# A decoder trunk with 32 experts: down-projection weights issued from GpSimd's queue instead of SyncE's

## What is computed

```python
def moe_ffn(xn, w_router, b_router, w1, b1, w2, b2):       # 256 + 16 tokens, top 4 of 32 experts
    logits = (tok_x @ w_router + b_router).astype(jnp.float32)
    top_logit, top_e = lax.top_k(logits, TOP_K)
    top_w = jax.nn.softmax(top_logit, axis=-1)
    ...
    def expert_block(blk):
        tok_blk, w_blk, e = blk
        hb = x_pad[tok_blk] @ w1[e] + b1[e]                 # w1[e]: 1024 x 2048, 8 MiB
        ob = clamped_swiglu(hb) @ w2[e] + b2[e]             # w2[e]: 1024 x 1024, 4 MiB
        return ob * w_blk[:, None].astype(ob.dtype)
```

## Time and profile before

| | |
|---|---|
| median of 3 runs | 1399.79 us (1399.71 to 1402.7) |
| profiled execution | 1400.83 us, of it 1399.0 us span |
| PE busy | 1337.8 us (96%) |
| DVE / ACT / POOL busy | 484.5 / 320.9 / 74.5 us |
| moved by DMA | 461.80 MB, mean 330 GB/s |
| SyncE's queue (q1) | 458.64 MB; GpSimd's queue (q0) 2.49 MB |
| granted TensorE clock | 1.00 of full in nearly the whole span |

### The profile page before, as it was taken

How to read it: one execution, slowest core, us unless ns; L and a number is a source line. 1 busy time by engine, 2 the same in 40 slices (tenths; PEclk the granted TensorE clock), 3 DMA queues, 4 the chain that set the end, 5 groups by cost and what they waited for, 6 DMA issues and landing times.

```text
span 1399.0 us, 18726 instructions
## 1 busy us (share of the span) xinstructions
PE 1337.8 (96%) x7131; PEld 652.9 (47%) x7131; DVE 484.5 (35%) x1217; ACT 320.9 (23%) x630; POOL 74.5 (5%) x88
## 2 busy tenths in 40 slices
PE   8999999999999999999999999999999999999995
PEld 5867778889994333333323222223222223333331
DVE  6847779998743212111211111111111211121112
ACT  4445547765321111111111011011001011011101
POOL 1000002322303000000000000000000000000000
PEclk9999999999999999999999999999999999999999
DMA  6332131334778899999999999999999999999995
GB/s 244 129 128 114 61 121 61 122 121 181 277 299 328 353 418 418 418 416 416 418 419 418 419 417 416 418 418 418 419 417 416 417 416 417 418 419 419 417 416 229
DMA packets 77410, 461.80 MB, mean 330 GB/s; under 512 B 6848, under 2 KB 6848, under 8 KB 41136
## 3 DMA queue, kind: packets, MB, share of 16 engines
q1 hardware_dynamic: 76608, 458.64, 80.8%
q0 software_dynamic: 752, 2.49, 0.5%
HBM read 460.05 MB, written 1.05 MB: 330 GB/s over the span
## 4 chain that ended last, share of the span: by engine, by line
PE 60%; DMA 19%; SPq 16%; DVE 2%; issue 2%; ACT 1%; ACTq 0%; DVEq 0%
PE bank L1299 57%; DMA ring<-w_dram 19%; SPq L405 9%; SPq L372 6%; PE bank L1614 1%; PE bank L1620 1%; PE bank L1425 1%; DMA work<-x_dram 0%; PE bank L1407 0%; PE bank L1636 0%; DVE split L887 0%; PE bank L1482 0%; DVE work L924 0%; PE bank L1326 0%; ACT split L553 0%
## 5 line engine op out<-in xcount | busy, mean ns | idle before, releaser
L1299 PE MATMUL bank<-ring,work 128*64 128x512 f32 (+3 forms) x2264 | 548.5, 591 | 34.5 <-DMA ring<-w_dram 32.1
L1299 PE MATMUL bank<-work 128*64 128x512 f32 (+7 forms) x2168 | 445.7, 558 | 6.2 <-issue 1.9
L1299 PEld LDWEIGHTS bank<-ring,work 128*64 128x64 f32 (+1 forms) x2264 | 176.7, 142 | 355.9 <-issue 259.7
L1299 PEld LDWEIGHTS bank<-work 128*64 128x64 f32 (+4 forms) x2168 | 151.3, 144 | 261.7 <-issue 245.6
L1247 DVE COPY work<-bank 128x256 f32<-128x256 f32 x32 | 13.6, 424 | 496.4 <-PE bank L1636 496.4
L1299 PE MATMUL bank<-hn_hi,split 128*128 128x256 f32 (+1 forms) x896 | 173.3, 289 | 0.9 <-DVE split L887 0.5
L1299 PEld LDWEIGHTS bank<-hn_hi,split 128*128 128x128 f32 x896 | 142.3, 190 | 1.7 <-issue 0.9
L1299 PE MATMUL bank<-hn_lo,split 128*128 128x256 f32 (+1 forms) x448 | 127.5, 285 | 0.0
L1221 DVE TENSOR_SCALAR work<-bank 128x256 f32<-128x256 f32 x64 | 24.2, 419 | 273.9 <-PE bank L1299 273.9
L887 DVE TENSOR_TENSOR split<-ring,split 128x1024 fp32r<-128x1024 f32 x80 | 99.1, 1240 | 26.0 <-ACT split L553 25.7
L739 ACT ACTIVATE work<-bank 128x512 f32<-128x512 f32 x32 | 19.1, 597 | 331.5 <-PE bank L1299 331.5
(11 more groups left out here) (250 smaller groups left out, 948.2 us busy)
## 6 DMA issues: line engine op xcount, KB each, us to landing
ring<-w_dram SPq DMA_DIRECT2D x256, 1024.0 KB, 21.4
work<-w_dram SPq DMA_DIRECT2D x128, 1024.0 KB, 19.9
ring<-slabs_dram SPq DMA_DIRECT2D x23, 2048.0 KB, 7.4
ring<-slabs_dram SPq DMA_DIRECT2D x2, 1152.0 KB, 5.2
ring<-slabs_dram SPq DMA_DIRECT2D x1, 1536.0 KB, 11.6
ring<-slabs_dram SPq DMA_DIRECT2D x1, 1280.0 KB, 8.4
work<-x_dram SPq DMA_DIRECT2D x2, 512.0 KB, 4.8
work<-x_dram POOLq DMA_DIRECT2D x2, 512.0 KB, 17.0
```

Of the source, the lines that this page charges most:

```text
L1299: return pe.matmul(o, lhsT, rhs, start=start, stop=stop)
```

## The change

The loads of w2 move from SyncE to GpSimd. In `first_expert` the w2 pieces of expert 0 go; GpSimd issues them between its `xn` instructions of the second token block, each pair after the same wait on the last slab of its slot. `load_down` is written on GpSimd, unchanged in its waits, and GpSimd runs it in one loop over experts 1 to 31 after its last work. SyncE issues w1 alone, in one loop, and the swapped order from expert 22 on goes with the w2 loads. The same holds for the further rounds. No buffer, semaphore or compute instruction changes.

```diff
             def first_expert(s, free):
                 sp.wait_ge(*free)
                 for k, (ks, _) in enumerate(W1_AT):
                     if ks == s:
                         sp.dma_start(w1_sb[k], w1[k * P:(k + 1) * P, :]).then_inc(w1_in[k], 16)
-                for j, (js, _) in enumerate(W2_AT):
-                    if js == s:
-                        sp.dma_start(w2_sb[j], w2[2 * j * P:2 * (j + 1) * P, :].rearrange("(j p) n -> p j n", j=2)).then_inc(w2_in[j], 16)
...
-            TURN = 11
...
-            def load_down(e, t):
-
-                for j in range(len(W2_AT)):
-                    if j < len(W2_AT) - 1:
-                        sp.wait_ge(down_used, (t - 1) * (len(W2_AT) - 1) + j + 1)
-                    else:
-                        sp.wait_ge(down_done, t)
-                    sp.dma_start(w2_sb[j], w2[bass.ds(e * DE + 2 * j * P, 2 * P), :].rearrange("(j p) n -> p j n", j=2)).then_inc(w2_in[j], 16)
-
...
-            for s in (2, 1):
-                first_expert(s, used[NEIGHBOURS[s][-1]])
+            sp.wait_ge(*used[NEIGHBOURS[1][-1]])
             load_w1(1, 5, True)
...
             load_up(2, 2, 0)
-            with sp.Fori(0, TURN) as i:
+            with sp.Fori(0, E // 2 - 2) as i:
                 for odd in (0, 1):
-                    e = 2 * i + odd
-                    load_up(e + 3, e + 3, 1 - odd)
-                    load_down(e + 1, e + 1)
-            for e in range(2 * TURN, E - 3):
-                load_down(e + 1, e + 1)
-                load_up(e + 3, e + 3, (e + 1) % 2)
-            load_down(E - 2, E - 2)
-            load_down(E - 1, E - 1)
+                    load_up(2 * i + odd + 3, 2 * i + odd + 3, 1 - odd)
+            load_up(E - 1, E - 1, 1)
...
             for b in range(2):
                 for n in range(2):
                     half = slice(n * 512, (n + 1) * 512)
+                    if b:
+                        s = 2 - n
+                        pool.wait_ge(*used[NEIGHBOURS[s][-1]])
+                        for j, (js, _) in enumerate(W2_AT):
+                            if js == s:
+                                pool.dma_start(w2_sb[j], w2[2 * j * P:2 * (j + 1) * P, :].rearrange("(j p) n -> p j n", j=2)).then_inc(w2_in[j], 16)
                     pool.wait_ge(h1_ready, 2 * b + n + 1)
...
+            def load_down(e, t):
+
+                for j in range(len(W2_AT)):
+                    if j < len(W2_AT) - 1:
+                        pool.wait_ge(down_used, (t - 1) * (len(W2_AT) - 1) + j + 1)
+                    else:
+                        pool.wait_ge(down_done, t)
+                    pool.dma_start(w2_sb[j], w2[bass.ds(e * DE + 2 * j * P, 2 * P), :].rearrange("(j p) n -> p j n", j=2)).then_inc(w2_in[j], 16)
+
+            with pool.Fori(1, E) as e:
+                load_down(e, e)
```

More of the change, by code:

```diff
@@ L437, in _ @@
                     load_up(1, r * E + 1, 1)
-                    load_down(0, r * E)
                     with sp.Fori(0, E // 2 - 1) as i:
@@ L442, in _ @@
                             load_up(e + 2, r * E + e + 2, odd)
-                            load_down(e + 1, r * E + e + 1)
-                    load_down(E - 1, r * E + E - 1)
             for n in range(2):
@@ L528, in _ @@
                 pool.tensor_scalar(xn[:, b, :], xn[:, b, :], rsh[:, b:b + 1], None, ALU.mult).then_inc(xn_scaled, 1)
+            def load_down(e, t):
[7 more added lines that the diff above has]
+                load_down(e, e)
+            pool.wait_ge(count_ready, 1)
+            cm = pool.value_load(cmax_i[0:1, 0:1], min_val=0, max_val=SEQ)
+            with pool.If(cm > SLOTS):
+                with pool.Fori(1, SEQ // SLOTS) as r:
+                    with pool.Fori(0, E) as e:
+                        load_down(e, r * E + e)
         @block.scalar
```

## The result

| | before | after |
|---|---|---|
| median of the runs side by side | 1401.24 us (1399.71 to 1403.13, 4 runs) | 1425.68 us (1417.33 to 1428.20, 4 runs) |
| profiled execution, of it span | 1400.83, 1399.0 us | 1417.33, 1415.6 us |
| PE busy | 1337.8 us | 1341.9 us |
| POOL busy | 74.5 us | 166.4 us |
| SyncE's / GpSimd's queue | 458.64 / 2.49 MB | 324.41 / 136.72 MB |

The ratio is 1.0167, with a 95% interval of 1.014 to 1.0193: slower, and by 1.7% where 0.4% was forecast (1405). The median lies 20.7 us above the forecast and 0.3 us inside the range of 1399 to 1426. The trace read here is of that shortest execution, so what it explains is a span of 1415.6 us and not the median.

The account below looks back on a forecast made before the run. DMA's rate (418 GB/s) bounds the kernel: down 28 starts at 1311.2, its expert ends at 1341.4, down 30 at 1379.3, plus 24.4 gives a span of 1403.7; with the median 0.8 above the span, 1405 (+0.4%), range 1399 to 1426.

Parts of the forecast that it names:

- rival (a): In each expert w2's ring runs dry for a moment or completions take no turn: 1410 to 1427, chance 0.30.
- (a)'s version with VectorE: VectorE's work at the down stage holds GpSimd's w2 request back by 1.4 us, half of that dry: span 1416.7.
- The bound: In the expert stage DMA's rate, 417 to 418 GB/s from 466 to 1381 us, sets the end, not TensorE.
- Rival (c): Two rings hide each other's gaps and raise the total DMA rate from 418 to 422 GB/s: 1396, chance 0.10.
- Issues at no cost: 128 issues move from SyncE to GpSimd, 1.35 us for two; SyncE's saving and GpSimd's cost are both 0.
- Split between two rings: In the expert stage w2 paces TensorE at 29.0 us an expert; w1's backlog grows 0.44 MiB an expert.
- Rival (b): Rings alternate in larger blocks, w2 gets half the rate and w1 paces from about expert 12: 1405, chance 0.12.
- Latency: Each expert's w2 request at 1.8 us brings data at 5.8, earlier data end at 6: ring just not dry.
- b: MiB of w1 asked for but not yet moved when a down stage starts; forecast 15 at expert 28.
- the formula: Span from w1 backlog at expert 28's down stage, where w1 is not late: 1436.8 - 2.51 x backlog in MiB.
- First experts: Periods of 27.4, 27.4, 29.7, then 29.05 us from expert 3; w1 backlog 3.7 and 4.0 MiB at experts 2, 3.
- End: Counted back from 1381: down 28 at 1311.2, down 30 ends at 1379.3, plus 24.4 gives a span of 1403.7.

Follow-up runs that it names:

- experiment 1: Kernel before without the swapped order, w1 of expert e+3 ahead of w2 of e+1 to the end, all on SyncE's queue: 1415.23 us, ratio 1.0102.
- experiment 2: Changed kernel with the queues exchanged, w2 on SyncE, w1 from expert 2 on GpSimd: 1410.35 us, ratio 1.0073 to the kernel before.
- experiment 6: Changed kernel with w2 laid out in 8 KB records instead of 4 KB, same bytes and sums: 1401.51 us, ratio 0.9998 to the kernel before.
- experiment 3: Changed kernel with GpSimd asking for each expert's first w2 piece only when two are used, 1.8 us later: 1430.81 us, ratio 1.0219 to the kernel before.
- the repeat: Changed kernel run again without any edit: 1424.32 us, ratio 1.0158 to the kernel before.
- experiment 4: Changed kernel with two unused filler matmuls on TensorE before the wait for the fourth w2 piece: 1419.83 us, ratio 1.0132 to the kernel before.
- the hold: Changed kernel where SyncE, from expert 22, holds w1 of e+3 until w2 of e+1 has landed: 1441.07 us, ratio 1.0296 to the kernel before.

## Why the prediction was right or wrong

**In all.** The range of 1399 to 1426 held the median of 1425.68 by 0.3 us, and it reached so far up only for the sake of rival (a), a ring that runs dry (1410 to 1427, chance 0.30). The forecast's own 1405, chance 0.40, missed it by 20.7 us. What came is (a)'s dry ring, with its sign that DMA goes quiet in the last 60 us (from 1353 on), and with it something that no rival had, the alternation of long and short experts. That the profiled span of 1415.6 lies beside the 1416.7 of (a)'s version with VectorE is luck: no delay by VectorE shows (last section).

**The bound: right.** DMA's rate sets the end, 417 to 418 GB/s with one queue or two. Rival (c), a higher sum with two rings, is out. The sign, the place (the end of the run) and the cause (how much w1 stock is left, the swapped order gone) were right; experiment 1 alone shows 14 us of it.

**Issues at no cost: right in length, wrong in effect.** An issue of GpSimd in the loop takes 0.72 us, two 1.43, near the 1.35 of the earlier trace rows, and the start of the stage is no later than before (L739 at 523.26 against 523.95). But the cost of w2's issues from GpSimd was not in their length.

**Split between two rings: right.** In the first part w2 pieces of an expert land 7.2 to 7.4 us apart, most of them within 7.20 and 7.24, forecast 7.25; no block of either queue shows. 34.6% of the bytes were forecast, 34.6 measured in experiment 2, 34.1 in the changed kernel. Rival (b), blocks, is out. It rested on a rule of the Trainium skill, page DMA: Bandwidth & Descriptors, section "Queues, rings and completion order", that an engine drains a whole packet of some 9 to 17 descriptors before it switches; the trace doesn't agree: taking turns with whole transfers would have given w2 its bytes early, at a period of 27.4 us, as the kernel with 8 KB records did in experiment 6, and not 34.1% of them.

**Latency: this is the first step that failed.** "The ring is just not dry" was a difference of two estimates: first data at 1.8 + 4, last data of the piece before at 6. GpSimd's queue in the changed kernel (start, us):

```profile
762.22 0.72 POOL L519 DMA_DIRECT2D ring<-w_dram  x1 [21.54 <-PE bank L1299]
763.93 0.72 POOL L519 DMA_DIRECT2D ring<-w_dram  x1 [0.99 <-PE bank L1299]
...
791.68 0.72 POOL L519 DMA_DIRECT2D ring<-w_dram  x1 [21.54 <-PE bank L1299]
793.39 0.72 POOL L519 DMA_DIRECT2D ring<-w_dram  x1 [0.99 <-PE bank L1299]
```

With down starting at 789.1, the first piece is used up at 790.9 and its successor issued at 791.68, 0.65 to 0.8 us later; that step from release to issue was left out of the sum. The 4 us from issue to data held (3.9): q0 from 795 to 795.5,

```profile
q0 software_dynamic: 7, 0.00, 0.8%
```

is seven completion records and no data, then data again from 795.5. Here, with the thin slices beside it, some 0.5 us of w2's rate are missing; over experts 4 to 14 it is 0.1 to 0.9 us, 0.4 on average. Rival (a) had this very mechanism, with "decides from 0.3 us". By its price of 0.4 MiB for each us the growth should fall from 0.44 to 0.28; it was 0.31 from expert 3 to expert 14. In experiment 2, where w2 comes from SyncE, it is 0.43, and in experiment 3, with a request 1.8 us later, nothing. But a growth of 0.31 by itself leads to b = 12.2 and to 1406, 2 us above the forecast's 1403.7. The slack of 0.2 us that wasn't there opened the door; most of the miss came through the next point.

**What no step had: the alternation and the clock.** The forecast had a stall of 1.6 us at the fourth piece in every expert; it was 1.95 on average up to 931 (29.35 - 27.40). TensorE at the change of character:

```profile
935.28 5.37 PE L1299 MATMUL bank<-ring,work 128*64 128x512 f32 x24
943.82 2.78 PE L1299 MATMUL bank<-ring,work 128*64 128x512 f32 x8 [3.17 <-DMA ring<-w_dram]
946.53 7.12 PE L1299 MATMUL bank<-work 32*64 32x512 f32 x24
```

The eight matmuls of the last piece take 2.78 us instead of 1.9, and the 24 after them 7.12, where the same group takes 4.67 at 1364.36: the half clock from 944.8 to 951.6, behind a pause of 3.17 us. What made this pause longer can be seen on GpSimd an expert earlier:

```profile
910.22 1.43 POOL L519 DMA_DIRECT2D ring<-w_dram  x2 [22.96 <-PE bank L1299]
912.21 0.72 POOL L519 DMA_DIRECT2D ring<-w_dram  x1 [0.56 <-issue]
```

An idle time of 22.96 instead of 21.54: this issue comes 1.42 us later than its like. From there on long and short experts alternate (34.07, 27.40, 32.81, 27.40, 31.15), stop doing so for three experts of 29.0 to 29.5, and alternate again from 1172 on. Of the six long ones five have a pause of 3.2 to 3.6 us and one of 1.9, and five are followed by half clock. That costs nothing in bytes, since DMA stays at 418, but w2's ring runs dry for longer (five times for 2.3 to 5.1 us), its share falls to 58.69 of 176.21 MB, 33.3%, and b stops growing. Against the 1406 of a growth that goes on, the swinging took some 9 us of the profiled execution, an estimate by the formula. The spread goes with it: over the eight executions of the changed kernel the mean granted clock was 0.994, 0.988, 0.982, 0.981, 0.980, 0.979, 0.978, 0.976 with spans of 1414.1, 1415.6, 1422.6, 1420.2, 1425.2, 1427.0, 1426.5, 1425.5 us. What sets the swinging off in one execution at 590 and in another at 940 stays open. The late issue stands right before it here and not in the repeat, so it isn't the only cause, and that it is one isn't shown. Nor is it shown how much of the swinging the half clock makes: experiment 4 took it away together with the pauses.

**First experts: right in kind.** Forecast periods of 27.4, 27.4, 29.7, 29.05; measured 27.40, 27.40, 28.57, 29.95, 28.98. In bytes b was 4.5 at expert 3, forecast 4.0; by the formula that is worth 1 us.

**End: right within 3 us.** 1418.2 by the formula, 1415.6 measured. From down 28 to the end of down 30 it took 59.5 us and not 63.6: expert 28's period had no wait (27.40, not 29.05), and expert 29's, in which no tokens are gathered any more, was 25.03 and not 27.4. After the end of down 30 the forecast has 24.4 us, measured 1389.38 to 1415.6 = 26.2. The last step of TensorE, answering to the earlier trace rows:

```profile
1382.34 7.04 PE L1299 MATMUL bank<-ring,work 128*64 128x512 f32 x32
...
1392.99 5.57 PE L1299 MATMUL bank<-ring,work 128*64 128x512 f32 x24 [0.56 <-issue]
1399.08 1.94 PE L1299 MATMUL bank<-ring,work 128*64 128x512 f32 x8 [0.53 <-DMA ring<-w_dram]
```

Down of expert 31 starts at 1392.99 and its last piece has to wait for a transfer: each w2 piece of expert 31 is asked for only when down 30 has used its predecessor, and DMA has nothing else to do by then.

**The sum.** Of the 24 us between the medians, 14 are the swapped order (experiment 1), 5 come back by two queues (experiment 2), and 15 go to w2's issues from GpSimd: to the dry ring, to the swinging and to the clock behind it. These are steps along one path of kernels; along another the shares could differ. The parts of the 15 are not cleanly separate; by the formula the dry ring alone is worth 2 us, and experiment 4 won 4 to 5 us back by taking away the pauses and the half clock.

## What to carry to other kernels

Here two DMA queues divided the rate by records, not by bytes (34.6% for w2 with 4 KB beside 8 KB, a half with 8 KB on both sides): before a stream moves to a queue of its own, count its records per byte against those of its neighbour, because that is its new priority, and a larger record raises it. A request chain with one set of buffers, where each load waits for the use of the one before it, lives on its latency from release to first data; if the slack there is a few tenths of a us, measure it rather than estimate it, since what hangs on it isn't the tenths but the stock of the other stream over all the rounds (in these kernels 12 MiB less what the rate moves in a period, each round). And an order written into one queue is worth something that two queues can't express: look first for what that order does at the end of the run, and don't rebuild it with a wait for a landing.

## What the runs showed of the hardware

- Engines took turns record by record between SyncE's and GpSimd's queue, completion records included: 12843 and 12558 packets of 8 and 4 KB between 590 and 930, w2's pieces 7.2 to 7.4 us apart.
- GpSimd's issue of 1 MiB took 0.72 us with 4 KB records and 0.54 us with 8 KB. First data came mostly 3.8 to 4.0 us after the issue onto an empty ring with SyncE's queue loaded, but 1.5 us after it on quiet engines (issue 438.53, data 440.0).
- The 57th and the 114th issue of the loop came 1.4 us late in the profiled executions of four kernels with 4 KB records of w2 on GpSimd's queue: the changed one (910.22 and 1335.68), the same again, with the filler, with the hold; in experiment 3 the same two (920.83 and 1345.41) were late as well. With 8 KB records it was the 110th, 2.7 us late, and in experiment 2, with w1 on GpSimd, the 114th and the 212th, 2.7 us late. 57 x 17 = 969, 110 x 9 = 990, 114 x 9 = 1026 and then 98 x 9 = 882 records an engine: it goes roughly with the number of records. The Trainium skill, page SBUF — State Buffer, section "SBUF: two separate sides", has GpSimd's descriptor writes held up while VectorE runs a two-port operation. The trace doesn't show it here: the issue at 1335.68 comes 1.9 us after the end of VectorE's burst (1333.76), and the first pieces of the other experts, issued with VectorE just as busy, have no delay. Nor does the time from issue to data: in experiment 3 VectorE's burst ends at 711.37, the issue comes at 711.98, and the first data 3.8 us later, as in the changed kernel, where the burst still runs at the issue. Why the count matters stays open.
- The granted clock fell to 0.50 for 3.4 to 10.2 us around pauses of TensorE of 1.9 to 3.6 us in the changed kernel, but not at each of them (none at 1062.33 to 1065.87, 3.54 us), and in the kernel with 8 KB records on two queues in every fourth expert behind a pause of 2.1 to 2.2 us (at 977.9, 1097.4, 1216.8, 1336.3), while other pauses of 2.1 us there had none. 71 waits of up to 0.7 us in experiment 1 left it at 1.00.
- 8 KB records for w2 raised the whole stream from 417 to 421 or 422 GB/s, less than the 425 of 8 KB packets alone in the earlier trace rows.
